# Expert mixer of a hybrid decoder: four prompt tiles take their activations from one dense product over the whole u table

## The reference, cut to what matters

```python
def one(xt):                                    # xt: a block of 128 tokens, normalized
    q = (xt @ w_query).reshape(blk, PEER_HEADS, 2, D_KEY // 2)
    s = jnp.einsum('thcd,cnd->thcn', q, sub_keys)
    s1, i1 = lax.top_k(s[:, :, 0], 16); s2, i2 = lax.top_k(s[:, :, 1], 16)
    cand = s1[..., :, None] + s2[..., None, :]  # 16 x 16 sums, the best 16 of them are taken
    sc, pos = lax.top_k(cand.reshape(blk, 8, 256), 16)
    idx = jnp.take_along_axis(cidx, pos, axis=-1)   # cidx = i1 * 128 + i2
    g = jax.nn.softmax(sc, axis=-1)
    act = gelu(jnp.einsum('thkd,td->thk', expert_u[idx], xt))
    return jnp.einsum('thk,thkd->td', g * act, expert_v[idx])

h = h + concat(y_ssm, y_diff) @ w_out           # the out projection
m = rmsnorm(h, g_ffn)
h = h + peer(m, ...)
h = h + (p @ w_ple) * sigmoid(rmsnorm(h, g_ple) @ w_ple_gate)   # the "end" of a tile
```

## Time and profile before

| what | us |
|---|---|
| median of 3 runs | 3607.18 |
| span of the profiled execution, first to last instruction | 3606.9 |
| `project` / `attend`, until | 505 / 745 |
| seeds (first product into the accumulators) of tiles 0, 1, 7, 8 | 871 / 1195 / 3173 / 3496 |

### The profile page before, as it was taken

How to read it: one execution, slowest core, us unless ns; L and a number is a source line. 1 busy time by engine, 2 the same in 40 slices (tenths; PEclk the granted TensorE clock), 3 DMA queues, 4 the chain that set the end, 5 groups by cost and what they waited for, 6 DMA issues and landing times.

```text
span 3606.9 us, 33674 instructions
## 1 busy us (share of the span) xinstructions
PE 2236.7 (62%) x9892; PEld 765.4 (21%) x9892; DVE 2216.6 (61%) x5337; ACT 1178.5 (33%) x3713; POOL 1268.5 (35%) x1243
## 2 busy tenths in 40 slices
PE   8999967868564554456355545634563654457775
PEld 3556533434110110011011101100110110012222
DVE  5325344626988558656855875586578557855555
ACT  2122214413423322422242242224223321354444
POOL 0000013202544444444444444444444443444342
PEclk9899978989675765567566757756675766577787
DMA  2211148875999999999999999999999999999997
GB/s 101 72 51 62 54 141 320 319 265 214 411 421 421 421 421 419 411 422 420 410 411 421 414 416 416 422 415 407 421 420 413 414 419 416 407 402 415 404 416 327
DMA packets 216450, 1260.05 MB, mean 349 GB/s; under 512 B 28677, under 2 KB 31450, under 8 KB 80882
## 3 DMA queue, kind: packets, MB, share of 16 engines
q0 software_dynamic: 165008, 1147.82, 77.6%
q1 hardware_dynamic: 46106, 101.76, 7.9%
q10 hardware_dynamic: 5152, 8.32, 0.7%
HBM read 1238.27 MB, written 24.05 MB: 350 GB/s over the span
## 4 chain that ended last, share of the span: by engine, by line
DMA 39%; PE 15%; DVE 8%; issue 7%; ACT 6%; POOL 3%; ACTq 0%; POOLq 0%; DVEq 0%; SPq 0%
DMA ex_ring<-in_expert_uv,ex_idx_cur 37%; PE ex_acc L2704 6%; PE ex_pk L2270 4%; POOL ex_ring L2526 3%; DVE ex_ring L2644 3%; PE ex_pk L1783 2%; ACT ex_diag L2582 2%; ACT ex_coef L2576 2%; DMA ex_ring<-in_expert_uv,ex_idx_few 1%; DVE ex_work L1927 1%; PE ex_pk L2138 1%; ACT ex_act_out L2573 1%; PE ex_pt L1753 1%; DVE ex_work L1920 1%; DVE ex_side_f L1932 1%
## 5 line engine op out<-in xcount | busy, mean ns | idle before, releaser
L2644 DVE CUSTOM_DVE_ANT_0 ex_ring<-ex_ring,ex_rows 128x1024 f32<-128x1024 f32 x1056 | 1291.1, 1224 | 849.6 <-DMA ex_ring<-in_expert_uv,ex_idx_cur 814.9
L2526 POOL DMA_INDIRECT ex_ring<-in_expert_uv,ex_idx_cur x1024 | 1136.1, 1109 | 1593.0 <-PE ex_acc L2704 1351.9
L2704 PE MATMUL ex_acc<-ex_ring,ex_diag 128*32 128x512 f32 x4096 | 828.0, 896 | 1107.8 <-ACT ex_diag L2582 1107.5
L2573 ACT ACTIVATE ex_act_out<-ex_dots 128x2 f32<-128x2 f32 x528 | 107.3, 203 | 1703.7 <-DVE ex_dots L2644 1703.1
L2704 PEld LDWEIGHTS ex_acc<-ex_ring,ex_diag 128*32 128x32 f32 x4096 | 97.0, 128 | 1771.5 <-ACT ex_diag L2582 1721.4
L2582 ACT ACTIVATE ex_diag<-ex_pick_row,ex_coef 128x32 f32<-128x32 f32 x1056 | 282.0, 314 | 50.5 <-ACT ex_coef L2576 1.5
L1783 PE MATMUL ex_pk<-ex_w,ex_aT 128*128 128x512 f32 x512 | 253.1, 637 | 0.0
L2576 ACT ACTIVATE ex_coef<-ex_act_out,ex_gate_cur 128x1 f32<-128x1 f32 x1024 | 245.6, 287 | 16.8
L340 PE MATMUL pj_bank<-pj_aT,pj_wbuf 128*128 128x512 f32 x512 | 226.7, 598 | 5.1 <-DVE pj_aT L529 5.1
L2270 PE MATMUL ex_pk<-ex_w,ex_aT 128*128 128x512 f32 x256 | 136.6, 680 | 26.4 <-issue 26.4
L1753 PE MATMUL ex_pt<-ex_wo,ex_aT 128*128 128x512 f32 x256 | 128.9, 647 | 9.1 <-DMA ex_wo<-in_w_out 9.1
(11 more groups left out here) (422 smaller groups left out, 2495.6 us busy)
## 6 DMA issues: line engine op xcount, KB each, us to landing
at_ring<-in_cache_kT SPq DMA_DIRECT2D x64, 256.0 KB, 9.4
at_ring<-in_cache_kT POOLq DMA_DIRECT2D x64, 256.0 KB, 6.0
at_ring<-in_cache_v SPq DMA_DIRECT2D x64, 256.0 KB, 8.9
at_ring<-in_cache_v POOLq DMA_DIRECT2D x64, 256.0 KB, 6.2
ex_ring<-in_expert_uv,ex_idx_cur POOLq DMA_INDIRECT x1024, 13.4
pj_wbuf<-in_w_in SPq DMA_DIRECT2D x6, 2048.0 KB, 10.5
ex_ring<-in_w_queryT SPq DMA_DIRECT2D x4, 2048.0 KB, 15.5
pj_aT<-in_xT_all SPq DMA_DIRECT2D x4, 1024.0 KB, 11.9
```

Of the source, the lines that this page charges most:

```text
L2526: pool.indirect_dma_start(ring[:, c % RING, :], None, t["expert_uv"], bass.IndirectOffsetOnAxis((idx_cur[k % 2] if k < LAST else idx_few)[ ...
L2573: act.activation(act_out[:, half, :], dots[:, half, :], ACT.Gelu).then_inc(gelu_done, 1)
L2644: dve.tensor_tensor_reduce(out=u, in0=u, in1=rows[:, j, :], scale=1.0, scalar=0.0, op0=ALU.mult, op1=ALU.add, accum_out=dots[:, q % HALVES ...
L2704: mm = pe.matmul(acc[n][quarter(j), :], diag[:, q % HALVES, p, :], ring[:, c % RING, D + n * 512:D + (n + 1) * 512], start=False, stop=las ...
```

## The change

In tiles 4 to 7 a call's activation is no longer computed from a gathered u row. Instead the product of the **whole** u table (16384 rows) with the 512 tokens of tiles 4 to 7 is computed once, as 128 blocks of 128 experts (`dense_tensor`, 8 products of 128x128 by 512 columns for a block), a few products after each call of tiles 1 to 3. ACT takes the gelu of each block (`dense_scalar`) and SP stores it to a new table `expert_vh` in HBM, whose row of 1536 floats holds: activations of tiles 4 and 5 (256 floats), the v row (1024), activations of tiles 6 and 7 (256). A call of tiles 4 to 7 gathers one contiguous piece of such a row, which holds v and the 32 activations that the call needs: 1280 to 1184 floats in tiles 4 and 7, 1152 to 1056 in tiles 5 and 6, 1168 floats (4672 bytes) on average. Its slot in the ring is smaller, so the ring has 12 slots there. DVE then makes the diagonal in one instruction of 128x32, and ACT does nothing for a call.

The v half of the table is copied into `expert_vh` during `project`, by 32 copies of 2 MB from HBM to HBM on SP's queue, 8 behind each of the last four weight loads.

Since the dense product needs the normalized tokens of tiles 4 to 7 before tile 1, all out projections and norms (order 2, 3, 1, 4, 5, 6, 7) run beside tile 0 (`ahead_*`). What later tiles need is parked in HBM: h, for tiles 1 to 3 the normalized rows, for tiles 2 and 3 their transposes, and for tiles 4 to 7 the transposes as one array of 2 MB. One of the 8 ring slots serves as a buffer for this, so tile 0 has 7. Beside tiles 1 to 6 only scores and search of the next tile remain (`look_*`). A tile's dense blocks and their loads use the place of `w_out` in SBUF, with three buffers for the loads and two for the results.

```diff
+N_EXP = KEYS * KEYS
+VH = D + 4 * P
+V_AT = 2 * P
+COPIES = 32
@@ project, SP
+                def copy_values(first, last):
+                    n = N_EXP // COPIES
+                    for i in range(first, last):
+                        part = slice(i * n, (i + 1) * n)
+                        sp.dma_start(t["expert_vh"][part, V_AT:V_AT + D], t["expert_uv"][part, D:2 * D]).then_inc(v_copied, 16)
...
                 for c in range(2, len(CHUNKS)):
                     weights(c)
+                    copy_values(8 * (c - 2), 8 * (c - 1))
                 few_loads(sp)
                 few_stores(sp)
+                sp.wait_ge(v_copied, 16 * COPIES)
@@ experts
+    FULL = 4
+    BLOCKS = N_EXP // P
+    BURST = 3
+    ORDER = [2, 3, 1] + list(range(FULL, LAST))
+    SMALL = VH - P * 2
+    SMALL_RING = RING * 2 * D // SMALL
+    def row_of(k, j):
+        at = k - FULL
+        if at < 2:
+            return at * P + j * SUB, V_AT + D
+        return V_AT, V_AT + D + (at - 2) * P + (j + 1) * SUB
...
+        def ahead_tensor(pe):
+            yield from pause(2)
+            for a in range(1, LAST + 1):
+                if a < LAST:
+                    pe.wait_ge(mix_in[(a + 1) % 2], 16 * (a // 2 + 1))
+                    pe.wait_ge(h1_ready, 2 * a)
+                    turn(pe, mix_of(a)).then_inc(turned, 1)
+                yield from pause(3)
+                if a > 1:
...
+                    turn(pe, mix_of(a - 1)).then_inc(m_turned, 1)
+                    if ORDER[a - 2] == 1:
+                        yield from pause(2)
+                        yield from score_tensor(pe, 1, BURST, 1)
...
+                yield from out_project(pe, a, BURST)
+                yield from pause(2)
+        def look_tensor(pe, k):
+            if k == 1:
+                yield from ahead_tensor(pe)
+            else:
+                yield from pause(2)
+                yield from score_tensor(pe, k, 1, 2)
...
+        def dense_tensor(pe):
+            done = 0
+            for b in range(BLOCKS):
+                pe.wait_ge(block_in[b % 3], 16 * (b // 3 + 1))
...
+                if b >= 2:
+                    pe.wait_ge(h_taken, b - 1)
+                for c in range(KT):
+                    mm = pe.matmul(pt[b % 2][:], block_buf[b % 3][:, c, :], mT4[:, c, :], start=(c == 0), stop=(c == KT - 1))
+                    if c == KT - 1:
+                        mm.then_inc(h_dots, 1)
+                    done += 1
+                    if done % BURST == 0:
+                        yield
+        def dense_scalar(act):
+            step, lag = 0, 2
+            for b in range(BLOCKS):
+                at = (KT * (b + 1) - 1) // BURST + lag
+                yield from pause(at - step)
+                step = at
+                act.wait_ge(h_dots, b + 1)
+                if b >= 2:
+                    act.wait_ge(h_out[b % 2], 16 * (b // 2))
+                act.activation(h_buf[b % 2], pt[b % 2][:], ACT.Gelu).then_inc(h_taken, 1)
+        def block_load(sp, b):
+            if b >= 3:
+                sp.wait_ge(h_dots, b - 2)
+            sp.dma_start(block_buf[b % 3], t["uT"][b * P:(b + 1) * P, :].rearrange("p (c e) -> p c e", e=P)).then_inc(
+                block_in[b % 3], 16)
+        def block_store(sp, b):
+            sp.wait_ge(h_taken, b + 1)
+            dst = bass.AP(t["expert_vh"].tensor, b * P * VH, [[VH, P], [V_AT + D, 2], [1, V_AT]])
+            sp.dma_start(dst, h_buf[b % 2].rearrange("p (a q) -> p a q", q=V_AT)).then_inc(h_out[b % 2], 16)
@@ POOL
+                        if c == FIRST_CALL[FULL]:
+                            for n in range(2):
+                                pool.wait_ge(h_out[n], 16 * BLOCKS // 2)
+                        if freed_by(c) is not None:
+                            pool.wait_ge(v_used, freed_by(c) // PAIR + 1)
...
+                        else:
+                            first, end = row_of(k, i % GRP)
+                            pool.indirect_dma_start(ring_flat[:, at:at + end - first], None, t["expert_vh"], index,
+                                                    element_offset=first).then_inc(came[slot], 16)
@@ DVE, a call of tiles 4 to 7
+                            landed(dve, c)
+                            if c % PAIR == 0:
+                                dve.wait_ge(v_used, q + 1 - HALVES)
+                            ins = dve.scalar_tensor_tensor(out=diag[:, q % HALVES, c % PAIR, :], in0=h_row(c),
+                                                           scalar=gate_cur[k % 2][:, i:i + 1], in1=pick_row[:],
+                                                           op0=ALU.mult, op1=ALU.mult)
+                            if c % PAIR:
+                                ins.then_inc(diag_v, 1)
```

More of the change, by code:

```diff
@@ L2462, in scale_gate, with beside @@
                 yield
-        def beside(k, front, few, end):
+        def beside(k, look, few, end, dense):
             if k == 0:
-                return [front(1), few]
-            return [front(k + 1) if k + 1 < LAST else end(k)]
+                return [look(1), few] if few is not None else [look(1)]
+            return [look(k + 1) if k + 1 < LAST else end(k)] + ([dense] if k < FULL else [])
         with nc.Block() as block:
@@ L2536, in _ @@
                 act.wait_ge(set_up, 2)
[L2537 to L2547 removed]
+                first_scalar(act)
                 fold_take(act, lambda out, src: act.activation(out, src, ACT.Copy), 0, range(4, 2 * PH))
@@ L2591, in _ @@
                                 for side in sides:
-                                    for _ in side:
-                                        pass
+                                    if side is not dense or k == FULL - 1:
+                                        for _ in side:
+                                            pass
                             for j in (0, 1) if q + 2 == end else (2, 3):
@@ L2597, in _ @@
                     for side in sides:
-                        for _ in side:
-                            pass
+                        if side is not dense:
+                            for _ in side:
+                                pass
                 out_scalar(act, LAST)
```

571 lines of the change are left out of this document (400 added, 171 removed).

## The result

The changed kernel takes 3472.18 us (median of 4 runs, 3467.06 to 3475.09) against 3608.38 for the kernel before on the same chip: a ratio of 0.962, 95% interval 0.9609 to 0.9632. It is faster by 136 us, where 33 were forecast. A second series of five runs gave 3475.70 and a ratio of 0.9635 (0.9621 to 0.9648).

A forecast was written before the change was run, and what follows sets the result against it. DMA was taken to bound the experts' stage except in `project`, with PE near in tile 7. Terms -522 + 20 + 48 + 331 + 52 + 38 = -33 from 3606.9 gave 3574 us, own range 3520 to 3640, overall 3440 to 3730.

The forecast's parts named there:

- Rival 1: Tiles 1 to 3: PE binds below its full clock, 3763 us at a fifth of pairs; chance 0.25 including waits for blocks.
- Rival 3: Tiles 4 to 7: gathers do not shrink with their bytes, POOL's long issue of 2.04 us binds; 3818 us, chance 0.03.
- Rival 2: All hides: copies unseen, tile 0 without stalls, DMA and PE averaged (-51), tiles 4 to 6 clean; 3453 us, chance 0.19.
- stated signs of a wrong forecast: Tiles 1 to 3: clock under 0.95 or DMA share under 0.9; diagonals 1.7 us apart; `project` ending at 505 or after 580.
- project, +38: In `project`, copies at 244 GB/s delay the sample tokens' loads to about 458 us, needed at 420.5; +38 us.
- Tile 0, +52: Tile 0: 40 us of extra loads and stores on full DMA, plus 12 for the boundary and jerks; bounds 36 and 95.
- both within 364: Tile 0: PE's and DVE's busy times, with the added out projections and norms, both fit within 364 us.
- Tiles 1 to 3, +331: Tiles 1 to 3: the dense product raises seed 1 to seed 4 from 979 to 1310 us.
- the slower engine counts: Tiles 1 to 3: dense pairs with a score take PE's 7.01 us, those without take DMA's 6.59 us.
- Tiles 4 to 6, -371: Tiles 4 to 6: smaller gathers cost 1.47 us per call instead of 2.49, less 20 us for PE; together -371 us.
- the +20 for PE at half clock: Tiles 4 to 6: pairs with a score product slow down as PE's clock lies between half and full; +20, bounds 0 and 70.
- Tile 7, -83: Tile 7: PE's products of the ends bind, 240 us against 323 before; gathers alone would give 192.

The follow-up runs named there:

- whole-row: Changed kernel with tiles 4 to 7 gathering the whole 6144-byte row of the new table, ring of 10 slots instead of 12: 3700.12 us.
- half-v runs: Changed kernel with tiles 4 to 7 gathering only half of each v row and using it twice (values wrong), one run: 3383.26 us.

## Why the forecast was right in its sign and wrong in its size

The exchange was as forecast: DMA time bought in tiles 4 to 7 and paid for in tiles 0 to 3. What the payment was made of was partly wrong. Rival 1 (PE below its full clock) did not come: the clock was 1.00 through tiles 1 and 2. Nor did the waits for blocks, up to 77 us, that the prediction worked out behind the rule of the Trainium skill ("DMA: Bandwidth & Descriptors", "Queues, rings and completion order") that a DMA engine takes turns between queues: a block's load took 8.6 us in the median from issue to landing, and PE was busy for 443.84 of tile 1's 446 us. Rival 3 fell with the whole-row and half-v runs. Rival 2, with its 3453 us, is nearer to the measured 3472 than the forecast. Two of its four parts came true, the copies that are not seen and tiles 4 to 6 with nothing added for PE; tile 0 without stalls did not, and of the 51 us for tiles 1 to 3 only 19 came, with PE as the bound. Of the stated signs of a wrong forecast one is there: `project` ends where it did before (the first load of `attend` leaves at 509.54 us, before at 507.93). The forecast missed by 102 us, by the pieces of the table. No single term stands for it: tiles 4 to 6 (56 us), `project` (35), tile 7 (26) and tiles 1 to 3 (19) came out better than summed, tile 0 (34) worse.

- **project, +38, measured +3.** The step that failed is the copies' price: the rate was taken from the fan and was 334 to 348 GB/s instead of 244. The repeated row, which the prediction had named as a possible reason and then left at the bound, is shown to slow such copies. The +3 is no effect: in eleven further executions that start alike, seed 0 came at 867 to 877 us.
- **Tile 0, +52, measured +86.** The transfers cost 58 us, not 40, and the holes 28, not 12. By bytes the forecast was nearly right (18.8 MB more, 45 us at 421 GB/s), and the rest is a lower rate: 370 GB/s at a share of 0.93 would be 398 at a full one, where tile 0 moved 410 before. The step "both within 364" added up PE's and DVE's busy time; it left out that both do the extra work in order, in front of the ring's accumulations. The ring of 7 slots did not cover it: with 6 it was 24 us worse, and with the work taken up two calls earlier 8 us better.
- **Tiles 1 to 3, +331, measured +312.** The price for PE is right within 3% (7.20 for 7.01 us with a score, 6.34 for 6.15 without). The step "the slower engine counts", with 32 x 6.59 by DMA, is wrong: PE sets those pairs too, at 6.34. That the sum for tile 1 still fits is luck: 32 x 7.20 + 32 x 6.34 = 433 us stands for the 435. Tiles 1 and 2 came out 5 us over the forecast, tile 3 9 us under, and the 15 us for reloads and PE's restarts do not show. DMA's own bound was 1215 us, not 1259. By that a block costs DMA about (1215 - 980) / 128 = 1.84 us, under the 2.14 that was summed; this is an estimate, since other loads of these tiles changed too.
- **Tiles 4 to 6, -371, measured -427.** The price per packet was right. Three terms were mis-sized: one mean size for all four tiles, while tiles 4, 5 and 6 have 4928, 4416 and 4416 bytes (11 us); the +20 for PE at half clock, which did not come, as DMA's share stayed 1.02 at a clock of 0.75 (20 us); and the 7 to 8 us per boundary, which I left standing (some 25 us over three tiles). Beyond the calls' own time tiles 4 and 5 have -1.7 and +1.4 us now, 8.5 and 7.1 before. These tiles no longer load their token rows; that this is why is argued, not shown. Tile 6 is some 16 us longer than that in both kernels. Its trace shows the loads of the ends' weights on SP's queue, which has 9.0% of the DMA engines' time in tile 6 and 1.4% in tile 5, 15 us more (before 5.4% and 1.2%, also 15).
- **Tile 7, -83, measured -109.** It takes 236 us where 240 were forecast. The step that failed is the base: I took 323 us from a stretch that ended at 3496, where the table of times before also has seed 8. Seed 8 stands at 3515, so the tile took 344.5 before, and the last piece of the table starts there.

What stays open: how one slot less comes to 24 us in tile 0, since the waits of several engines grow together; and what in the parts of PE's work in tile 0 gives the 13 us.
